# Joint attention: value pages issued from GpSimd's queue and awaited in pairs

## The reference

```
def _diff_combine(s, lam):
    p = jax.nn.softmax(s, axis=-1)
    B, _, Q, K = p.shape
    p = p.reshape(B, H_C, 2, Q, K)
    return p[:, :, 0] - lam * p[:, :, 1]

def diff_attn_cached(q, k, v, kp, vp, lam):      # samples
    s_p = jnp.einsum('bqhd,bkhd->bhqk', q, kp).astype(F32) * scale
    s_n = jnp.einsum('bqhd,bkhd->bhqk', q, k).astype(F32) * scale
    ...
    a = _diff_combine(jnp.concatenate([s_p, s_n], axis=-1), lam)
    return (jnp.einsum('bhqk,bkhe->bqhe', a[..., :P], vp.astype(F32))
            + jnp.einsum('bhqk,bkhe->bqhe', a[..., P:], v.astype(F32)))

kp = cache_k[o][page_table].reshape(Bs, past, 2 * H_C, HD_C)
vp = cache_v[o][page_table].reshape(Bs, past, H_C, 2 * HD_C)
```

## Time and profile before

| | us |
|---|---|
| median of 3 runs (2607.79 to 2609.01) | 2608.84 |
| the profiled execution, its own time | 2608.57 |
| its span, first to last instruction | 2606.4 |
| TensorE busy | 2479.2 |
| VectorE busy | 1306.1 |
| ScalarE busy | 892.1 |
| GpSimd busy | 408.8 |

### The profile page before, as it was taken

One profiled execution on the slowest core, in us unless ns is written; L12 is line 12 of the kernel. 1 busy time (PEld: TensorE's weight loads), 2 busy tenths in 40 slices (PEclk: granted clock), 3 DMA queues, 4 the chain that ended last, 5 costly groups with the idle time before them and its releaser, 6 DMA issues.

```text
span 2606.4 us, 47024 instructions
## 1 busy us (share of the span) xinstructions
PE 2479.2 (95%) x17168; PEld 1959.7 (75%) x17168; DVE 1306.1 (50%) x2218; ACT 892.1 (34%) x2136; POOL 408.8 (16%) x242
## 2 busy tenths in 40 slices
PE   7999999999993999979999999998999999999988
PEld 6898898898883777758878888875666666666666
DVE  4656555323333466663235343335666666666653
ACT  4122121111111333332232111145666666666621
POOL 4224224323400000000004242200000000000021
PEclk9999999999996899989999999999999999999999
DMA  5233223224227398892133424259999999999962
GB/s 164 77 108 107 82 80 106 80 68 129 77 73 187 110 286 282 269 309 89 73 115 92 122 90 133 82 185 395 411 391 408 397 396 394 408 395 390 391 192 73
DMA packets 332228, 535.42 MB, mean 205 GB/s; under 512 B 30069, under 2 KB 241794, under 8 KB 328810
## 3 DMA queue, kind: packets, MB, share of 16 engines
q1 hardware_dynamic: 328962, 524.16, 57.5%
q10 hardware_dynamic: 3080, 8.82, 0.9%
HBM read 432.20 MB, written 100.56 MB: 204 GB/s over the span
## 4 chain that ended last, share of the span: by engine, by line
PE 87%; DVE 5%; DMA 3%; SPq 2%; issue 1%; ACT 1%; ACTq 1%; POOL 0%; DVEq 0%; POOLq 0%
PE at_ring L2838 8%; PE p_col L572 5%; PE p_col L574 5%; PE p_col L573 5%; PE p_gm L2275 4%; PE p_gm L2276 4%; PE p_gm L2277 4%; PE at_ssc L2867 4%; PE at_ring L2856 4%; PE p_row L613 4%; PE p_row L615 4%; PE p_row L614 4%; PE at_sc L2806 3%; PE at_ring L2828 3%; PE oa_out L1833 2%; PE oa_out L1835 2%
## 5 line engine op out<-in xcount | busy, mean ns | idle before, releaser
L2838 PE MATMUL at_ring<-ident,at_kp 128*128 128x128 f32 x2048 | 268.3, 277 | 14.1 <-DMA at_kp<-in_cache_k 9.1
L2838 PEld LDWEIGHTS at_ring<-ident,at_kp 128*128 128x128 f32 x2048 | 223.9, 141 | 58.3 <-issue 36.9
L572 PE MATMUL p_col<-h_hi,p_wqk 128*128 128x352 f32 x768 | 251.4, 327 | 1.1 <-DVEq L801 1.1
L574 PE MATMUL p_col<-h_hi,p_wqk 128*128 128x352 f32 x768 | 247.3, 322 | 0.0
L573 PE MATMUL p_col<-h_lo,p_wqk 128*128 128x352 f32 x768 | 247.0, 322 | 0.0
L2941 ACT ACTIVATE at_kT<-at_ring 128x512 f32<-128x512 f32 x384 | 218.2, 597 | 71.3 <-PE at_ring L2838 69.3
L613 PE MATMUL p_row<-p_wvz,h_hi 128*128 128x512 f32 x512 | 203.8, 398 | 3.6 <-ACT p_vst L696 3.6
L2275 PE MATMUL p_gm<-p_whl,h_hi 128*128 128x512 f32 x512 | 202.1, 395 | 0.9 <-DVE h_lo L2415 0.6
L615 PE MATMUL p_row<-p_wvz,h_lo 128*128 128x512 f32 x512 | 202.1, 395 | 0.0
L614 PE MATMUL p_row<-p_wvz,h_hi 128*128 128x512 f32 x512 | 201.3, 393 | 0.0
L2277 PE MATMUL p_gm<-p_whl,h_lo 128*128 128x512 f32 x512 | 199.6, 390 | 0.0
(11 more groups left out here) (405 smaller groups left out, 4866.2 us busy)
## 6 DMA issues: line engine op xcount, KB each, us to landing
at_kp<-in_cache_k SPq DMA_DIRECT2D x256, 512.0 KB, 7.4
at_vp<-in_cache_v SPq DMA_DIRECT2D x256, 512.0 KB, 7.5
s_qk<-p_res SPq DMA_DIRECT2D x32, 528.0 KB, 2.8
p_wst<-in_w_in_a SPq DMA_DIRECT2D x32, 512.0 KB, 3.9
p_wst<-in_w_in_a SPq DMA_DIRECT2D x64, 256.0 KB, 2.9
mx_qk<-s_qk SPq DMA_DIRECT2D x16, 1024.0 KB, 9.5
p_wst<-in_w_in_c SPq DMA_DIRECT2D x64, 256.0 KB, 4.6
s_v<-p_vst SPq DMA_DIRECT2D x64, 128.0 KB, 2.8
```

What stands on the lines that cost most here:

```text
L572: pe.matmul(out[:, r, 0:TN], wx[:, 0, k, :], h_hi[:, k, at], start=k == 0, stop=False)
L574: last = pe.matmul(out[:, r, 0:TN], wx[:, 1, k, :], h_hi[:, k, at], start=False, stop=k == KD - 1)
L2838: last = pe.transpose(bank("key", n, f)[:, h * PAGE:(h + 1) * PAGE], kp[n % 2][k][:, tile:tile + P], c.ident[:])
```

## The change

The value pages of groups 2 to 63 move from SyncE's stream to GpSimd's; those of groups 0 and 1 stay on SyncE, ahead of the loop. GpSimd issues them in a loop over the steps, after its leave of the earlier stage, with the same waits for free slots, and computes a head's inverse square root after the pages of its step. The eight semaphores of value pages, one for each slot and page, become four for pairs: `v_first` for groups 0 and 1 and `v_loaded` for the others, and TensorE waits once for two pages. Nothing that is computed changes.

```
-        k_loaded, v_loaded = st.sems("k_loaded", 2 * GP), st.sems("v_loaded", 2 * GP)
+        k_loaded, v_first, v_loaded = st.sems("k_loaded", 2 * GP), st.sems("v_first", GP), st.sems("v_loaded", GP)
...
-        def page(sp, cache, pages, loaded, n, k):
+        def page(eng, cache, pages, loaded, n, k):
             at = pt[0:1, n * GP + k:n * GP + k + 1]
-            number = sp.value_load(at, min_val=0, max_val=N_POOL - 1)
-            sp.dma_start(pages(n, k), cache[0, bass.ds(number, 1)].rearrange("a k h d -> (a k) (h d)")).then_inc(
-                loaded[n % 2 * GP + k], 16)
+            number = eng.value_load(at, min_val=0, max_val=N_POOL - 1)
+            eng.dma_start(pages(n, k), cache[0, bass.ds(number, 1)].rearrange("a k h d -> (a k) (h d)")).then_inc(loaded, 16)
...
-            page(sp, g["cache_v"], lambda n, k: vp[:, n % 2, k, :], v_loaded, n, k)
+            page(sp, g["cache_v"], lambda n, k: vp[:, n % 2, k, :], (v_first if n < 2 else v_loaded)[n % 2 * 2 + k // 2], n, k)
...
                     key(sp, s + 2, 0)
-                if s >= 3:
-                    for k in range(GP):
-                        value(sp, s - 1, k)
                 if s + 2 < NG:
...
                 for k in range(GP):
-                    pe.wait_ge(v_loaded[n % 2 * GP + k], 16 * (n // 2 + 1))
+                    if k % 2 == 0:
+                        pe.wait_ge((v_first if n < 2 else v_loaded)[n % 2 * 2 + k // 2], 32 * max(1, n // 2))
...
             leave(c, pool, 4)
             clear_behind(c, pool, 4)
-            for hd in range(HC):
-                pool.wait_ge(sq_ready, hd + 1)
-                pool.tensor_tensor(rstd[:], o_ms[:, hd % 2, :], half[:], ALU.pow).then_inc(rooted, 1)
+            for s in range(3, NG + 2):
+                if s <= NG:
+                    for k in range(GP):
+                        value(pool, s - 1, k)
+                if s > NB and s % NB == 1:
+                    hd = (s - 1) // NB - 1
+                    pool.wait_ge(sq_ready, hd + 1)
+                    pool.tensor_tensor(rstd[:], o_ms[:, hd % 2, :], half[:], ALU.pow).then_inc(rooted, 1)
```

More of the change, by code:

```diff
@@ L2684, in key @@
                 wait_fill(sp, "key", n - 2, 2 * k + 1)
-            page(sp, g["cache_k"], lambda n, k: kp[n % 2][k][:], k_loaded, n, k)
+            page(sp, g["cache_k"], lambda n, k: kp[n % 2][k][:], k_loaded[n % 2 * GP + k], n, k)
         def value(sp, n, k):
```

## The result

| | us |
|---|---|
| changed kernel, median of 4 runs (2621.59 to 2626.08) | 2625.38 |
| kernel before beside it, median of 4 runs (2606.27 to 2609.01) | 2608.32 |
| ratio, with its 95% interval | 1.0060 (1.0049 to 1.0072) |
| the profiled execution of the changed kernel, its own time | 2626.08 |

A forecast was written before the change was run, and what follows sets the result against it. TensorE was taken as the bound, with the DMA engines close behind at 96%. Step 5 wait 8.5 + slow clock 1.5 - end 1.0 = +9.0 us on 2608.57 us, stated as 2617.5 us, range 2609 to 2638.

The forecast's parts named there:

- my first case: Whole kernel: one wait for value pages in step 5 and nothing else, +4 to +16 us; chance 0.55.
- The first value pages of GpSimd come late: Step 5: pages issued behind GpSimd's leave make PE wait 8.5 us, plus 1.5 us of slow clock, 10.0 us.
- Middle: Steady attention steps: moving page issues from SyncE to GpSimd costs 0, since PE waits for no page there.
- the rival of less DMA rate: From 1810 us on: two queues together move less than the kernel's 397 GB/s, 2622 to 2650 us; chance 0.20.
- its form of key pages behind a prompt head: Middle: key pages behind a prompt head's 1.5 MB come late, 12.4 us becoming 17 at worst; within the 0.20.
- The square root behind four page issues: Each head on GpSimd: root ends at 1857 to 1864 us, VectorE may wait; 0 for PE, upper end 14 us.
- Pairs: TensorE's waits for two pages at once: no cost where pages are in time; late pages' extra issue counted elsewhere.
- The end: Last four value pages, in their own queue, need not wait for every weight: 1 us gain, ends 3.0 either way.

The follow-up runs named there:

- e2: Changed kernel with the value pages of the last three groups (61 to 63) issued by SyncE again: 2624.60 us, ratio 1.0063.
- e9: The changed kernel measured once more, unedited, beside two versions of its end: 2625.64 us, ratio 1.0055 to the kernel before.
- e10: Changed kernel with the value pages of the last three groups back on SyncE, measured a second time: 2624.21 us, ratio 1.0055.
- e11: Changed kernel with only the prompt rows of the output projection loaded one step earlier: 2622.37 us, ratio 1.0045.
- e1: Changed kernel with GpSimd issuing the value pages of groups 2 and 3 before its leave of the earlier stage: 2614.67 us, ratio 1.0016.
- e5: e1 with the prompt rows po_y and po_z loaded one step earlier, in step 60 and not 61: 2611.40 us, ratio 1.0007.
- e4: Kernel before, all pages on SyncE, with value-page semaphores and waits in pairs: 2610.23 us, ratio 1.0004.
- e7: e5 with the key pages of group 3 issued ahead of the last stores of the stage before: 2611.31 us, ratio 1.0006.
- e3: e1 with the value pages of the last three groups back on SyncE: 2611.00 us, ratio 1.0007.
- e6: Kernel before, all pages on SyncE, with group 3's key pages issued ahead of the last stores of the stage before: 2602.63 us, ratio 0.9971.

## Why the prediction was right or wrong

The direction, the place of the main cost and the range were right; the likeliest time was 7.9 us too low, and one term had the wrong sign. The time alone would not have told the cases apart: 2625.4 us is at the upper end of my first case (2612 to 2625) and inside that of the DMA rate (2622 to 2650). It is the traces that speak for the first.

**The first value pages of GpSimd come late: right, 10.0 us forecast, 10.4 to 12.5 measured.** The traces of the five kernels with this start give, from group 0 to group 10, +10.4, +11.1, +12.0, +12.5 and +10.8 us (changed kernel, e2, e9, e10, e11), and the medians say the same: changed kernel less e1, 10.7 us; e11 less e5, 11.0 us. Within it several numbers were off, and it is luck that they nearly cancelled (10.7 us in the first profile). The first page went out 2.0 us after the clear began, not 0.9. It landed later than my 4.8 us: PE gets the pair at 1816.9 us, 6.2 us after the second page was issued at 1810.76, and over the first twelve pages the landing took 5.7 to 7.2 us. So the first wait was 8.2 us and not 6.3. Against that pages go out every 1.16 us, not 1.6, and the first pair's matmuls took 1.93 us at half clock where I had 1.0, so the second pair was 0.54 us late and not 2.2. The clock took 1.9 us, the upper end of my 0 to 1.9: behind 8.2 us without a matmul both halves ran at 0.50.

**Middle: right, 0.** 563.63 and 563.66 us. At 1.16 us a page GpSimd needs 4.6 us of each step of 11.25 us. The two queues together reach 410 to 415 GB/s in their best slices, as the earlier trace rows: the rival of less DMA rate fell, and so did its form of key pages behind a prompt head. Of that form the first half did happen: the slowest key page took 16.8 us instead of 12.4 (I had 17 at worst) and the head's own load 14.3 us instead of 10.6 (medians), but the cushion of 21 us held. The Trainium skill (DMA: Bandwidth & Descriptors, Issuing engines are not separate DMA queues) said that a second issuer only saves issue time, and the trace agrees for the sum of bytes: 399 GB/s from 1900 to 2300 us, 398 before. The rule of the Trainium skill on DMA engines 7 and 15 (the same page, Latency and other measured facts) cost nothing in this sum; no run here shows the single engines.

**The square root behind four page issues: right, 0.** GpSimd and VectorE at the first head, each in order of time:

```profile
1871.96 0.53 POOL L2679 DMA_DIRECT2D at_vp<-in_cache_v  x1 [1.09 <-issue]
1872.51 1.68 POOL L3039 TENSOR_TENSOR at_rstd<-at_o_ms,at_half 128x8 f32<-128x8 f32 x1
```

```profile
1873.46 0.69 DVE L3096 COPY at_kT<-at_ring 128x512 f32<-128x512 f32 x1 [0.81 <-PE at_ring L2834]
1874.22 1.23 DVE L3163 TENSOR_TENSOR at_o<-at_o,at_rstd 128x1024 f32<-128x1024 f32 x1
```

The root ends at 1874.19 us and VectorE, busy until 1874.15, takes it at 1874.22 without a wait. It was forecast to end at 1857 to 1864; with the 15.3 us by which the stage stands later here that is 1872 to 1879, and it ends at 1874.2. It came out even, with nothing to spare, and VectorE waits for it at no head. The upper end of 14 us took 2 us a head, for which I had no row.

**Pairs: right, 0** within what was measured (e4, +0.7, interval -1.3 to +3.4 us).

**The end: wrong, -1.0 forecast, about +3 measured.** The step that failed is "I take a third of the 3.0 us as gain". I put the gain on the value pages of the last group and named the rows of the prompt only as something that takes turns with these pages. I never asked who waits for the rows. The value pages did gain a little in the first profile (1.4 us of wait instead of 3.0), but PE came late to them there; with all of them on GpSimd the same wait was 3.2 to 4.1 us in the other five profiles (e1, e5, e7, e9, e11), no gain. What weighed was the other direction: value pages of group 61, which stood behind the rows in one queue, now run beside them. DMA queues in 25 us around these loads, before (2440 to 2465 us) and changed (2455 to 2480 us):

```profile
DMA packets 5833, 9.02 MB, mean 361 GB/s; under 512 B 278, under 2 KB 4118, under 8 KB 5829
...
q1 hardware_dynamic: 5829, 8.98, 102.4%
...
po_z<-s_z SPq DMA_DIRECT2D x2, 512.0 KB, 8.6
```

```profile
DMA packets 5783, 8.87 MB, mean 355 GB/s; under 512 B 265, under 2 KB 4105, under 8 KB 5779
...
q1 hardware_dynamic: 4630, 4.63, 58.8%
q0 software_dynamic: 1149, 4.19, 43.9%
...
po_z<-s_z SPq DMA_DIRECT2D x2, 512.0 KB, 14.5
```

The total is the same, but SyncE's queue, with packets of 1.0 KB on average, had 102% of the engines and now has 59%. So the rows land in 14.5 us instead of 8.6, VectorE waits 4.1 us for them, and the delay passes through ScalarE to PE. My upper end, a loss of 3.0, came close by luck: I had the rows take turns with the value pages, but made the value pages the ones that come late. The price is 3.3 us in the medians, twice (e1 less e5, e9 less e11), and 2.2 and 3.8 us by the means of the same runs; in the traces the end is longer by 2.8 (changed kernel), 3.3 (e1) and 1.3 us (e9) than before. That the rows are late and VectorE waits is shown; that it costs about 3 us is well supported in the kernel without the wait in step 5 (e1 against e3 and e5), and less so in the changed kernel itself.

The parts of what was measured: 10.7 us at the start (changed kernel less e1), 3.3 at the end (e1 less e5), and 1.9 us that remain in e5 against before (interval -0.5 to +4.2). They add up to 15.9 us by their making, since each is the next kernel's difference; the ratio of the changed kernel gives 15.7. The last piece is not resolved.

## What to carry to other kernels

A transfer that moves to another engine's stream inherits everything that stands ahead of it there. Look for the marks and drains of that stream first; here one such line was two thirds of the loss, and moving it behind the first eight pages removed it. Where it went it cost GpSimd 12 us, since its drain then waited for those pages to land; that is free only as long as nobody needs the next ones. And one queue is also an order: before splitting it, list the transfers that were early only because others stood behind them, and ask of each who waits for it; moving the rows one step ahead gave back what the second queue had cost them, and keeping one queue with the urgent pages in front (e6) was worth 6.9 us, where the second queue bought nothing, the matmul engine being the bound.

## What the runs showed that I had not expected

- A page of 512 KB issued by GpSimd takes 0.53 us of its time and comes every 1.15 to 1.16 us while nothing holds it, hardly more than SyncE's 1.11.
- A drain on GpSimd lasted until its own transfers had landed: 12.3 to 13.1 us in five kernels, with its end 0.3 us behind the last landing each time.
- The same kernel gave 14.5 and 8.1 us for the landing of the same rows in two executions, with equal issue times relative to the pages around them (the issue itself took 1.40 us and 0.56 us of SyncE). What decides it is open.
